# Turning the mixers' results group by group, and sending each batch's scores behind the batch ahead of it

## The reference, cut to what matters

```
(qa, ka, va, qh, fh, ih, gh, qkm, vm, om, im, fm) = split_cols(h @ w_in, IN_SIZES)
y_attn  = sliding_window_attention(qa, ka, va, sinks)            # 16 heads of 64  -> 1024 columns
y_hgrn  = rms_norm(o_h, hgrn_gain) * silu(gh)                    # 4 heads of 128  ->  512 columns
y_mlstm = sigmoid(om) * o_m                                      # 4 heads of 128  ->  512 columns
y = concatenate([y_attn, y_hgrn, y_mlstm]);  x = x + y @ w_out
x = x + PEER(rms_norm(x))        # rows of peer_u and peer_v are fetched by index
```

## Time and profile before

| | us |
|---|---|
| median of 3 runs (lowest to highest) | 3619.2 (3610.1 to 3627.41) |
| the profiled execution, its own time | 3624.84 |
| its span, first to last instruction | 3622.6 |
| PE busy (share of the span) | 2871.8 (79%) |
| DVE busy | 2196.6 (61%) |
| ACT busy | 760.8 (21%) |
| mean granted TensorE clock | 0.958 |

### The profile page before, as it was taken

The page is one execution under the profiler, slowest core; times in us unless marked ns, Lnnn a source line. Parts: engine busy times, 40 slices in busy tenths (PEclk is TensorE's granted clock), DMA queues, the critical chain, the costliest instruction groups (busy, mean ns, idle before and its releaser), DMA issues.

```text
span 3622.6 us, 31542 instructions
## 1 busy us (share of the span) xinstructions
PE 2871.8 (79%) x10443; PEld 1662.0 (46%) x10443; DVE 2196.6 (61%) x3080; ACT 760.8 (21%) x1189; POOL 1392.2 (38%) x1028
## 2 busy tenths in 40 slices
PE   7999938878787788777789999388777877787776
PEld 7887824433342343232388778234333423332322
DVE  6765576665656566655566655765656655665655
ACT  4344411111111111111143444011111111111111
POOL 0000046545545555544400000555545555555443
PEclk9999969999999999999999999699999999999999
DMA  5434579999999999999944344899999999999998
GB/s 190 142 127 150 197 284 408 414 418 413 416 419 414 404 419 419 415 416 415 420 145 141 127 165 161 338 411 417 414 412 411 419 421 408 415 416 418 413 419 362
DMA packets 239655, 1243.78 MB, mean 343 GB/s; under 512 B 24680, under 2 KB 33072, under 8 KB 107440
## 3 DMA queue, kind: packets, MB, share of 16 engines
q0 software_dynamic: 147456, 1073.81, 72.1%
q1 hardware_dynamic: 92080, 168.51, 13.6%
HBM read 1240.14 MB, written 2.10 MB: 343 GB/s over the span
## 4 chain that ended last, share of the span: by engine, by line
DMA 36%; PE 32%; DVE 17%; issue 8%; DVEq 3%; ACT 2%; POOL 2%; POOLq 0%; SPq 0%; ACTq 0%
DMA work<-in_peer_v_dram,idx_v 21%; PE PS L502 16%; DMA work<-in_peer_u_dram,idx_u 14%; PE PS L801 13%; DVE work L1702 6%; POOL work L1140 2%; DVE xs L1715 2%; DVE lo L1268 2%; DVEq L1379 1%; ACT hi L860 1%; DVE gain L1646 1%; DVE gain L1647 1%; ACT work L934 1%; DVE gain L1680 0%; DVE gain L1649 0%
## 5 line engine op out<-in xcount | busy, mean ns | idle before, releaser
L801 PE MATMUL PS<-work,diag 128*128 128x512 f32 x3968 | 1855.5, 615 | 640.0 <-DMA work<-in_peer_v_dram,idx_v 455.9
L1702 DVE CUSTOM_DVE_ANT_0 work<-work,hn 128x2048 f32<-128x2048 f32 x512 | 1164.3, 2291 | 851.2 <-DMA work<-in_peer_u_dram,idx_u 820.7
L801 PEld LDWEIGHTS PS<-work,diag 128*128 128x128 f32 x3968 | 739.6, 195 | 1726.0 <-issue 1302.8
L1140 POOL DMA_INDIRECT work<-in_peer_u_dram,idx_u x512 | 775.4, 1514 | 1501.2 <-DVEq L1686 941.6
L1140 POOL DMA_INDIRECT work<-in_peer_v_dram,idx_v x512 | 616.6, 1204 | 700.0 <-PE PS L801 565.4
L1069 ACT ACTIVATE diag<-cst,act_k 128x128 f32<-128x128 f32 x496 | 190.1, 398 | 1383.9 <-PE PS L801 1374.0
L502 PE MATMUL PS<-hT_hi,hi 128*128 128x256 f32 x1024 | 306.6, 299 | 43.8 <-DVE lo L1602 16.2
L502 PE MATMUL PS<-hT_lo,hi 128*128 128x256 f32 x1024 | 295.8, 289 | 0.0
L502 PE MATMUL PS<-hT_hi,lo 128*128 128x256 f32 x1024 | 295.7, 289 | 0.0
L502 PE MATMUL PS<-hi,hT_hi 128*128 128x512 f32 (+1 forms) x704 | 278.5, 396 | 9.9 <-ACT work L904 4.1
L502 PE MATMUL PS<-hi,hT_lo 128*128 128x512 f32 (+1 forms) x704 | 272.1, 386 | 0.0
(11 more groups left out here) (251 smaller groups left out, 1615.1 us busy)
## 6 DMA issues: line engine op xcount, KB each, us to landing
raw<-in_w_in_dram SPq DMA_DIRECT2D x40, 1024.0 KB, 5.0
gain<-in_w_in_dram SPq DMA_DIRECT2D x38, 1024.0 KB, 5.0
raw<-in_peer_query_dram SPq DMA_DIRECT2D x24, 1024.0 KB, 16.1
raw<-in_w_out_dram SPq DMA_DIRECT2D x16, 1024.0 KB, 5.1
gain<-in_w_out_dram SPq DMA_DIRECT2D x16, 1024.0 KB, 5.1
work<-in_peer_query_dram SPq DMA_DIRECT2D x8, 1024.0 KB, 7.4
work<-in_peer_u_dram,idx_u POOLq DMA_INDIRECT x512, 14.3
work<-in_peer_v_dram,idx_v POOLq DMA_INDIRECT x512, 14.0
```

The lines of the kernel that those rows point to most:

```text
L801: mm = pe.matmul(PS[:, j, :], diag[:, n % RING, :], vrow[n % RING][:, j * 512:(j + 1) * 512], start=(k == 0), stop=(k == (TOPK - 2 if last ...
L1140: pool.indirect_dma_start(out=dst, out_offset=None, in_=tables[table], in_offset=bass.IndirectOffsetOnAxis(ap=idx, axis=0)).then_inc(loade ...
L1702: dve.tensor_tensor_reduce(r, r, hn[:, b, :], 1.0, 0.0, ALU.mult, ALU.add, pre[:, b, k:k + 1]).then_inc(u_free.sem, 1)
```

## The change

It has two parts. In the **attention**, `scores(n+1)` now follow `turn_probs(n)` behind piece 25+2n, and `attend(n)` stands alone behind piece 26+2n. `soft(n+1)` writes `probs`, so it waits for `probs_turned(n)`. DVE's list becomes `take_probs(n)`, `soft(n+1)`, `convolve(n-1)`, `take_attended(n)`, with each `split_to` one piece lower. ACT rounds one piece between the exponentials and the copy to `probsT`, and `drain(6)` stands ahead of `batch_exps(3)`. In the **turning**, group 0 is transposed behind `hgrn_attend` (piece 41), group 1 behind piece 42, group 2 behind piece 44 and group 3 behind piece 45, all through banks 6 and 7. ACT and DVE take each group once the piece that last reads the old group of `hT` is used; pieces 44 to 47 wait for their own group alone.

```
-            def turn_mixed(l):
-                for f in range(8):
-                    g, b = f // NB, f % NB
-                    if f >= 4:
-                        pe.wait_ge(turned_dve.sem, turned_dve.upto(l, 8 + f - 3))
-                    if g == 3 and b == 0:
-                        pe.wait_ge(mixed.sem, mixed.upto(l, 2))
-                    transposed(f, hn, g, b)
-                pe.wait_ge(turned_dve.sem, turned_dve.upto(l, 16))
...
-                def batch_step(n):
+                def probs_step(n):
                     def go():
-                        if n > 0:
-                            attend(n - 1)
-                        if n < NBATCH:
-                            scores(n)
+                        turn_probs(n)
+                        if n + 1 < NBATCH:
+                            scores(n + 1)
                     return go
...
-                for n in range(NBATCH + 1):
-                    steps[24 + 2 * n] = batch_step(n)
-                    if n < NBATCH:
-                        steps[25 + 2 * n] = lambda n=n: turn_probs(n)
+                steps[24] = lambda: scores(0)
+                for n in range(NBATCH):
+                    steps[25 + 2 * n] = probs_step(n)
+                    steps[26 + 2 * n] = lambda n=n: attend(n)
...
-                steps[41] = hgrn_attend
+                def turn_mixed(g):
+                    if g >= 2:
+                        pe.wait_ge(mixed.sem, mixed.upto(l, g - 1))
+                    for b in range(NB):
+                        if g > 0:
+                            pe.wait_ge(turned_dve.sem, turned_dve.upto(l, 8 + NB * (g - 1) + b + 1))
+                        transposed(2 + b, hn, g, b)
+                def hgrn_step():
+                    hgrn_attend()
+                    turn_mixed(0)
+                steps[41] = hgrn_step
+                steps[42] = lambda: turn_mixed(1)
+                steps[IN_PIECES] = lambda: turn_mixed(2)
+                steps[IN_PIECES + 1] = lambda: turn_mixed(3)
...
-                pe.wait_ge(mixed.sem, mixed.upto(l, 1))
-                turn_mixed(l)
-                pe.wait_ge(drained.sem, drained.upto(l, NS))
+                pe.wait_ge(drained.sem, drained.upto(l, NS - 1))
                 for p in range(IN_PIECES, PIECES):
                     o = p // 4 - NS
+                    if p % 4 == 0 and o == 1:
+                        pe.wait_ge(drained.sem, drained.upto(l, NS))
                     if p % 4 == 0 and o >= 2:
                         pe.wait_ge(out_taken.sem, out_taken.upto(l, o - 1))
+                    if o == 0:
+                        pe.wait_ge(turned_dve.sem, turned_dve.upto(l, 8 + NB * (p % 4 + 1)))
                     project(l, p)
+                    steps.get(p, nothing)()
...
 (ACT, batch_exps)
                     a.then_inc(exped.sem, 1)
+                    round_to(28 + 2 * n)
                     act.wait_ge(probs_turned.sem, probs_turned.upto(l, n + 1))
...
                 batch_exps(2)
+                drain(6)
                 batch_exps(3)
-                drain(6)
...
-                round_to(45)
+                def take_mixed(g):
+                    act.wait_ge(pieces_used.sem, pieces_used.upto(l, IN_PIECES - 3 + g))
+                    for b in range(NB):
+                        take_tile(turned.upto(l, 8 + NB * g + b), 2 + b, g, b)
+                round_to(44)
                 act.wait_ge(hgrn_out.sem, hgrn_out.upto(l, 1))
                 act.activation(osq..., ACT.Square).then_inc(hgrn_sq.sem, 1)
+                take_mixed(0)
                 act.wait_ge(hgrn_var.sem, hgrn_var.upto(l, 1))
                 act.activation(hss[:], hss[:], ACT.Sqrt).then_inc(hgrn_std.sem, 1)
+                round_to(45)
+                take_mixed(1)
                 drain(10)
-                for f in range(8):
-                    take_tile(turned.upto(l, 8 + f), f, f // NB, f % NB)
+                round_to(47)
+                take_mixed(2)
+                round_to(48)
+                take_mixed(3)
...
 (DVE)
-                    split_to(27 + 2 * n)
+                    split_to(26 + 2 * n)
                     dve.wait_ge(scored.sem, scored.upto(l, n + 1))
+                    if n > 0:
+                        dve.wait_ge(probs_turned.sem, probs_turned.upto(l, n))
...
+                soft(0)
                 for n in range(NBATCH):
-                    soft(n)
+                    take_probs(n)
+                    if n + 1 < NBATCH:
+                        soft(n + 1)
                     if 1 <= n < 5:
                         convolve(n - 1)
-                    take_probs(n)
                     take_attended(n)
```

More of the change, by code:

```diff
@@ L1480, in take_probs @@
                     hs = slice(h0, h0 + nh)
-                    split_to(28 + 2 * n)
+                    split_to(27 + 2 * n)
                     dve.wait_ge(exped.sem, exped.upto(l, n + 1))
@@ L1489, in take_attended @@
                     b, h0, nh = BATCHES[n]
-                    split_to(29 + 2 * n)
+                    split_to(28 + 2 * n)
                     dve.wait_ge(attended.sem, attended.upto(l, n + 1))
@@ L1567, in _, with take_mixed @@
                 dve.tensor_scalar(hss[:], hss[:], 1.0 / P, EPS, ALU.mult, ALU.add).then_inc(hgrn_var.sem, 1)
-                split_to(45)
+                def take_mixed(g):
+                    for b in range(NB):
+                        take_tile(turned_act.upto(l, 8 + NB * g + b), 2 + b, g, b)
+                take_mixed(0)
                 dve.wait_ge(hgrn_std.sem, hgrn_std.upto(l, 1))
@@ L1577, in _ @@
                 dve.drain().then_inc(mixed.sem, 1)
+                split_to(45)
+                take_mixed(1)
                 split_to(46)
@@ L1582, in _ @@
                 dve.drain().then_inc(small_used.sem, 1)
-                split_to(IN_PIECES + LOS)
-                for f in range(8):
-                    take_tile(turned_act.upto(l, 8 + f), f, f // NB, f % NB)
+                take_mixed(2)
+                split_to(47)
+                take_mixed(3)
                 def split_first(j):
```

## The result

The changed kernel takes 3586.73 us (median of 4 runs, 3582.79 to 3590.82); the kernel before, on the same chip, 3621.14 us (4 runs, 3610.10 to 3627.41). The ratio is 0.9909, with a 95% interval of 0.9888 to 0.9929: 34.4 us less. Run again beside the experiments it gave 0.9905 (0.9890 to 0.9920). The forecast was 29 us less, 3590 us, in a range of 3578 to 3607.

A forecast was written before the change was run, and what follows sets the result against it. PE was taken to bound the mixers' part of the dense stage, DMA the gathers. Terms: 14.4 + 9.3 + 3.9 + 2.5 - 1 = 29.1 us saved, from 3619.2 to 3590 us, range 3578 to 3607.

The forecast's parts named there:

- Waits removed: In the attention, PE's waits for exponentials, a drain and a split go: 14.4 us over both layers.
- the turning's term: At the turning of hT, 8.98 us shrink to four transpose blocks of 4.3 us: 9.3 us saved in both layers.
- Cost of the four blocks: At the turning, eight transposes between two pieces cost PE 1.08 us, four such blocks 4.3 us a layer.
- check on piece 44: Sign in the trace: piece 44 starts some 154.5 us behind the mixers' start, instead of 167.4 us.
- Clock: Slow PE clock goes: 3.9 us behind the turning in both layers, 2.5 us (half of 5.0) in the attention.
- New waits: Output pieces 46 to 48 may wait for their weights, piece 48 tightest: 1 us lost, bounds 0 and 8.
- Cover: In the attention, DVE keeps 1.9 us of room per period and ACT's extra rounding stays hidden: cost 0.
- Late weights (1): At pieces 46 to 48, weights come a split late each, returning 13.8 us: 3604 us; 12%.
- Clock at the blocks (2): At the turning's four transpose blocks the clock sinks, so only 13 us are saved: 3606 us; 9%.
- The end that doesn't follow (3): PE waits in the dense stage's tail or the gathers take the time back: 3617 us, no change; 6%.
- ACT's rounding (4): Rounding ahead of the copy to probsT delays attend; with transfers of 15 us, slower at 3630 us; 4%.

The follow-up runs named there:

- e7_back: The changed kernel with two orders put back: ACT's drain(6) behind batch_exps(3), DVE's split of piece 26 ahead of the first softmax; 3594.33 us.
- e5_turns: The changed kernel with 32 transposes instead of 8 in each of turn_probs' twelve blocks; 3619.50 us in one run.
- e1_attn: The kernel before with only the attention's part of the change, the turning left as it was; 3597.37 us, ratio 0.9939.
- r_before2: The kernel before, unchanged, in a further profiled execution; the stretch averaged 536.0 us over three executions of before.
- e3_keys: The changed kernel with the sixteen loads of the sub-keys issued as two; 3584.13 us, ratio 0.9910.
- r_after: The changed kernel, unchanged, in a second profiled execution; the stretch took 501.1 and 501.2 us in the two of after.
- e8_dve: The changed kernel with one added reduction of 2.2 us on DVE ahead of each take_attended; 3583.02 us.
- e6_dve: The changed kernel with two added reductions, 8.9 us together, on DVE ahead of each take_attended; 3652.04 us.

## Why the prediction was right, and where its sum was not

Right in sign, in mechanism, and by 3 us in the time. Term by term, with the three executions of before (538.1, 535.9 and 534.1 us, mean 536.0) and the two of after (501.1 and 501.2): 34.9 us for the stretch, which agrees with the medians' 34.4.

1. *Waits removed.* Forecast: 14.4 us in the attention, and within the turning's term 2 x (2.7 + 1.4) = 8.3, less 1 for new waits: 21.7 us less idle. Measured: 25.3 us on average before (24.0 to 26.2), 2.8 to 2.9 after, 22.5 less. Right, and each wait went where the text said.
2. *Cost of the four blocks.* 1.08 us each were forecast; in the rows above a piece with its block takes 345.91 - 339.57 = 6.34 us, and 24 products at their spacing of 0.227 us are 5.45, so a block lengthens PE's path by 0.89 us. The sum had it 0.8 us a layer too dear. The check on piece 44 (154.5 us behind the part's start; it was 334.2 - 185.1 = 149.1) had a slip besides: it charged all four blocks, and two of them stand behind piece 44. The other 3.2 us of that miss are mostly slow clock: 1.5 us were allowed for the first layer's mixers, where the table has 3.3. The sum isn't touched by the slip.
3. *Clock.* This is the term that was mis-sized, in both of its halves. Behind the turning I took the 3.9 us of the one execution as what each run pays; over eight such turnings 5.9 us were paid in all, 0.7 each, so about 1.5 us for the two layers. In the attention's part I took half of 5.0 us (one stretch was overlooked; the table has 3.3 + 2.6 = 5.9 for that execution), because one of the slow stretches followed no wait but `spread_m`, and concluded that it would stay. It didn't: the part lost 5.7 us a run (2.9 a layer over twelve), and without waits nothing. Behind `spread_m` the clock fell, with waits ahead, in about half of the layers, and again when `e7_back` put back two waits of 0.9 us. So the row directly ahead of a slow stretch doesn't tell what it belongs to. By these counts waits that ended 40 us earlier have a share in it; the stretch in `e5_turns`, with no such wait, says that they are not all of it. Together the clock's two terms make 7.2 us by these sums, where 6.4 stood in the forecast: the errors nearly cancelled.
4. *What is left.* The busy time fell by 12.4 us on average (510.7 to 498.3). 7.2 are those slow products. The transposes at the turning were slowed too (the second sixteen took 2.91, 2.91 and 3.30 us where the clock fell, for 2.45 at full clock; up to 3.68 in `e1_attn`), 0.6 us a run. That leaves 4.6 us, and little of it can be the clock. In `r_before2`'s first layer the granted clock was down in one stretch alone (PE columns):
```profile
188.57:278.50 89.93, 83.20 (x522) 1.00 0.39 133
278.50:281.95 3.45, 3.45 (x13) 0.51 0.00 0
281.95:453.89 171.94, 166.38 (x865) 1.00 0.50 171
```
   That stretch cost 3.45 x 0.49 = 1.7 us. The layer's busy time is 253.0 us, so 251.3 without it, against 249.2 in the changed kernel: 2.1 us a layer, 4.3 in both, that the clock doesn't explain. Some 1.6 of these are the turning (its two sixteens take 1.91 + 2.45 = 4.4 us at full clock, the four blocks 4 x 0.89 = 3.6); the rest I put down to the dearer first products behind a wait, which I have not counted one by one.
5. *New waits.* 1 us forecast, 0.83 + 0.62 measured, at the piece named, behind the queue named; `e3_keys` shows that SP's issues were the cause. In `r_after` it was 1.5 us in one layer and nothing in the other.
6. *Cover.* DVE's room is over 2.2 us (`e8_dve`), 2.4 by the estimate from `e6_dve`; the forecast had 1.9. ACT's rounding ahead of the copy cost nothing: no wait at `attend`.
7. *Rivals.* Late weights (1): three pieces late by one split, 13.8 us; one piece, 1.5 us. Clock at the blocks (2): the Trainium skill (TensorE: Matmul & The Clock Gate, Part 4: PE-mode transpose) would have it fall there; no block did that here, at 8 transposes or at 32. The end that doesn't follow (3): the first gather moved by 16.7 us, with the stretch. ACT's rounding (4): no sign of it.

So the 5.8 us that the forecast of 29.1 fell short of the stretch's 34.9 are, by these terms: 0.8 us of idle time, 1.4 of clock (7.8 for 6.4), and 3.6 in the busy time of the turning and the restarts, where the sum had 9.3 - 8.3 = 1.0 us. That last term is the largest miss, and the forecast had nothing for the restarts. That the time was met to within 3 us owes something to luck as well, since the clock's two halves were off in opposite directions.

## What to carry over

Where PE is the bound and others feed it, put a whole piece of its own work between a question to a neighbour and the use of the answer. Count a PE wait at more than its length, since slow stretches of about 1.7 us go with such waits, at times pieces later; but give that term a range, for one profile's slow stretches are a draw while its waits are not. And price an added operation by the shape of its tile in the trace.

## What the hardware showed that I had not expected

- The granted clock of one program differs between executions at the same instruction and the same wait (behind the waits of 2.75 us at the turning it was 0.50 and 0.55 in one execution and 1.00 in another).
- With waits of 0.9 us a slow stretch came over 40 us later, at `spread_m`, in both layers of `e7_back`; of the layers without waits in that part ten had none, and of `e5_turns`' two one had it. Why, no run here shows.
- When the clock falls within the turning, the transposes end later and the wait behind them is shorter (1.41 instead of 1.73 us), so a slow clock partly hides in a smaller wait: only busy plus idle time can be compared.
- Two loads of 512 KB cost SP 0.99 us of issuing, sixteen of 64 KB 8.11 us; the single load behind them then took 3.57 us to issue instead of 0.43. The time of the whole group fell from 8.6 to 4.6 us, not to 1.4.
